# Queries and keys of a head group computed together by seven half products, with x parked in DRAM

## The reference

```python
cond = silu(c)
sh1, sc1, g1, sh2, sc2, g2 = split(cond @ w_ada + b_ada, 6)
h = rms_norm(x, norm_mix) * (1 + sc1) + sh1
y = dilated_mixture_attention(h, attn_w_in, attn_w_out)
x = x + g1 * y
h = rms_norm(x, norm_ffn) * (1 + sc2) + sh2
x = x + g2 * conv_ffn(h, ffn_w_up, ffn_conv_w, ffn_conv_b, ffn_w_down)
return rms_norm(x, norm_final)
```

## Time and profile before

| | |
|---|---|
| median of 3 runs | 942.18 us (941.74 to 942.84) |
| the profiled execution | 943.8 us, its span 942.0 us |
| TensorE (PE) busy | 922.9 us, 98%, 5828 matmuls |
| weight loads (PEld) | 797.4 us, 85% |
| VectorE (DVE) | 579.1 us, 61% |
| ScalarE (ACT) | 445.5 us, 47% |
| GpSimd (POOL) | 51.2 us, 5% |
| granted TensorE clock | 0.997 of full speed |
| DMA | 121.4 MB, 129 GB/s in the mean |

### The profile page before, as it was taken

The page is one execution under the profiler, slowest core; times in us unless marked ns, Lnnn a source line. Parts: engine busy times, 40 slices in busy tenths (PEclk is TensorE's granted clock), DMA queues, the critical chain, the costliest instruction groups (busy, mean ns, idle before and its releaser), DMA issues.

```text
span 942.0 us, 16200 instructions
## 1 busy us (share of the span) xinstructions
PE 922.9 (98%) x5828; PEld 797.4 (85%) x5828; DVE 579.1 (61%) x1261; ACT 445.5 (47%) x810; POOL 51.2 (5%) x75
## 2 busy tenths in 40 slices
PE   7999999999999999999999999999999999999995
PEld 6688888888888888888888888889999999888884
DVE  3444664745746557457565667888888888633325
ACT  7245435435344444453444555555666556432222
POOL 2000000000000000000000001411112111000000
PEclk9999999999999999999999999999999999999998
DMA  9865442343415332334242222367888876522302
GB/s 307 255 192 144 134 135 85 95 135 112 134 50 150 115 115 85 115 112 135 67 135 68 67 64 72 107 153 188 187 192 178 186 183 144 179 90 89 111 0 90
DMA packets 166528, 121.38 MB, mean 129 GB/s; under 512 B 4662, under 2 KB 149198, under 8 KB 166478
## 3 DMA queue, kind: packets, MB, share of 16 engines
q1 hardware_dynamic: 161088, 111.17, 39.1%
q0 software_dynamic: 5184, 9.44, 6.7%
q10 hardware_dynamic: 206, 0.08, 0.0%
HBM read 109.13 MB, written 2.10 MB: 118 GB/s over the span
## 4 chain that ended last, share of the span: by engine, by line
PE 90%; DVE 4%; DMA 2%; SPq 1%; ACT 1%; POOL 1%; issue 1%; DVEq 0%; POOLq 0%; ACTq 0%
PE bank L786 13%; PE bank L788 13%; PE bank L787 13%; PE bank L998 6%; PE bank L996 6%; PE bank L999 6%; PE bank L1045 4%; PE bank L1047 4%; PE bank L1046 4%; PE bank L870 3%; PE bank L846 3%; PE bank L813 2%; PE bank L879 2%; PE bank L806 1%; PE bank L881 1%; PE bank L880 1%
## 5 line engine op out<-in xcount | busy, mean ns | idle before, releaser
L1412 DVE TENSOR_TENSOR wl<-raw,wh 128x1024 fp32r<-128x1024 f32 (+1 forms) x127 | 150.5, 1185 | 176.9 <-ACT wh L1103 175.9
L786 PE MATMUL bank<-hh,wl 128*128 128x512 f32 x544 | 215.2, 396 | 0.0
L788 PE MATMUL bank<-hl,wh 128*128 128x512 f32 x544 | 212.0, 390 | 0.0
L787 PE MATMUL bank<-hh,wh 128*128 128x512 f32 x544 | 211.8, 389 | 0.0
L1103 ACT ACTIVATE wh<-raw 128x1024 fp32r<-128x1024 f32 (+1 forms) x127 | 130.4, 1027 | 60.3 <-PE bank L1047 50.9
L786 PEld LDWEIGHTS bank<-hh,wl 128*128 128x128 f32 x544 | 102.1, 188 | 23.9 <-issue 2.7
L788 PEld LDWEIGHTS bank<-hl,wh 128*128 128x128 f32 x544 | 102.1, 188 | 21.7
L787 PEld LDWEIGHTS bank<-hh,wh 128*128 128x128 f32 x544 | 102.2, 188 | 20.1
L996 PE MATMUL bank<-th,wl 128*128 128x256 f32 x304 | 84.8, 279 | 1.0 <-ACT p_copy L1280 0.9
L998 PE MATMUL bank<-th,wh 128*128 128x256 f32 x304 | 85.4, 281 | 0.0
L999 PE MATMUL bank<-tl,wh 128*128 128x256 f32 x304 | 85.1, 280 | 0.0
(11 more groups left out here) (221 smaller groups left out, 1600.2 us busy)
## 6 DMA issues: line engine op xcount, KB each, us to landing
raw<-in_attn_w_in SPq DMA_DIRECT2D x72, 512.0 KB, 3.8
ada_raw<-in_w_ada SPq DMA_DIRECT2D x16, 1024.0 KB, 5.4
raw<-in_ffn_w_up SPq DMA_DIRECT2D x25, 512.0 KB, 4.1
sums<-in_ffn_w_up SPq DMA_DIRECT2D x36, 256.0 KB, 3.3
raw<-in_ffn_w_down SPq DMA_DIRECT2D x17, 512.0 KB, 3.3
sums<-raw POOLq DMA_DIRECT2D x27, 256.0 KB, 4.9
ada<-in_w_ada SPq DMA_DIRECT2D x16, 256.0 KB, 6.8
raw<-in_attn_w_out SPq DMA_DIRECT2D x8, 512.0 KB, 3.6
```

The lines of the kernel that those rows point to most:

```text
L786: nc.tensor.matmul(bank[:], wl[:, slot, t], xh[:, t], start=(t == 0), stop=False)
L787: nc.tensor.matmul(bank[:], wh[:, slot, t], xh[:, t], start=False, stop=False)
L788: last = nc.tensor.matmul(bank[:], wh[:, slot, t], xl[:, t], start=False, stop=(t == KT - 1))
L1412: nc.vector.tensor_tensor(dst, src, high.bitcast(F32), ALU.subtract).then_inc(done, 1)
```

## The change

1. **Blocks instead of q and k strips.** In pairs 1 to 7 the six strips of q and k become three blocks, one per group, of seven products each (`block`, `block_product`). The three value strips stay, and come first. Pair 0 stays in strips.
2. **Weight sums.** For each block, `pair_sum` holds four half tiles: two are loaded from the keys' weights and added to by DMAs on GpSimd's queue, two are made by DVE (`sum_pair`). They are split into high and low part like the other weights (`split_block`: SUM0, DIRECT, SUM1 of 1024 elements and LAST of 512 per partition).
3. **Input forms.** `token_forms` makes four forms of h (1024 elements a partition each) in the first pair on DVE, and ACT and DVE split them into `mh` and `ml`.
4. **Space.** `mh` lies where `xT` lay. So `xT` is written to DRAM (`x_held`, 2 MB) behind the loads of the first pair, and read back in four DMAs after the last block; the attention's residual add waits for these (`x_back`). `q_t` and `k_t` have one buffer instead of two, the output's copy uses `p_t` instead of `o_a`, and there is a fourth raw tile, `raw_3`.
5. **Order.** All programs are written out for the seven pairs. The attention of the pair before is called from `visit` between products. Each product writes one of two halves of the two `proj` banks, and so waits for ACT's copies (`copy_block`, `take_block`) and DVE's additions (`add_block`).
6. **Prologue.** The first chunk's modulation is done between the transposes of x, ACT copies its rows before the first weight split, and the dummy transposes become 5 + 12, 10 and none, where there were 16, 16 and 10.

The core of the diff:

```diff
-QKV_STRIPS = PAIRS * STRIPS
+QKV_STRIPS = STRIPS + GROUPS * (PAIRS - 1)
+BLOCKS = GROUPS * (PAIRS - 1)
...
+        def block_banks(g):
+            bank, other_bank = unit_bank(GROUPS + g), unit_bank(GROUPS + g + 1)
+            return bank[:, 0:HALF], other_bank[:, HALF:T], other_bank[:, 0:HALF]
...
+            sp.wait_ge(start_taken, KT)
+            sp.dma_start(x_held, xT[:]).then_inc(x_saved, 16)
...
+            sp.wait_ge(block_prod, PRODUCTS * BLOCKS)
+            sp.wait_ge(x_saved, 16)
+            for i in range(KT // 2):
+                sp.dma_start(xT[:, 2 * i:2 * i + 2], x_held[:, 2 * i:2 * i + 2]).then_inc(x_back[i], 16)
...
+                    pool.wait_ge(pair_in[0], 16 * (i + 1))
+                    pool.wait_ge(raw_in[r_two], 16 * count_two)
+                    nc.gpsimd.dma_start(pair_sum[:, 0], raw_of(r_two)[:, HK:KT], accum_op=ALU.add).then_inc(pair_added[0], 16)
...
+            pe.wait_ge(start_taken, KT + 2)
+            hold(5)
             start_columns(0)
-            pe.wait_ge(start_taken, KT + 2)
-            hold(16)
-            start_highs((0, 1), range(RING))
+            hold(12)
+            for s in range(RING):
+                start_highs((0, 1), (s,))
             start_modulation(1)
             start_lows((0, 1), range(RING))
             start_columns(1)
-            hold(16)
+            hold(10)
...
             start_lows((2, 3), (2, 3))
-            hold(10)
...
+            def block(n, g, visit):
+                i = block_of(n, g)
+                r, q, z = block_banks(g)
+                early, late = slice(0, HALF), slice(HALF, T)
+                pe.wait_ge(block_l[DIRECT], i + 1)
+                if g == 0:
+                    pe.wait_ge(strip_taken, strips_before(n) + 2)
+                else:
+                    pe.wait_ge(block_added, 3 * i)
+                block_product(r, 0, 0, hh[:, 0:HK, early], hl[:, 0:HK, early], True, False)
+                visit(g, 1)
...
+                block_product(q, 1, 0, mh[:, 0], ml[:, 0], True, False)
+                pe.wait_ge(block_copied, 3 * i + 1)
+                block_product(r, 1, 1, mh[:, 1], ml[:, 1], False, False)
+                pe.wait_ge(block_copied, 3 * i + 2)
+                block_product(z, 0, 1, hh[:, HK:KT, early], hl[:, HK:KT, early], False, True)
+                visit(g, 4)
+                pe.wait_ge(block_l[SUM1], i + 1)
+                pe.wait_ge(block_copied, 3 * i + 3)
+                block_product(r, 2, 0, mh[:, 2], ml[:, 2], False, False)
+                visit(g, 5)
+                pe.wait_ge(block_added, 3 * i + 1)
+                block_product(q, 2, 1, hh[:, HK:KT, late], hl[:, HK:KT, late], False, True)
+                pe.wait_ge(block_l[LAST], i + 1)
+                pe.wait_ge(block_added, 3 * i + 2)
+                block_product(r, 3, 0, mh[:, 3], ml[:, 3], False, True)
...
+            def sum_pair(n, g):
+                nc.vector.tensor_tensor(pair_sum[:, 1], pair_sum[:, 0], one[:, 0:HK], ALU.add).then_inc(pair_sums, 1)
+                dve.wait_ge(pair_sums, 2 * i + 1)
+                nc.vector.tensor_tensor(pair_sum[:, 3], one[:, HK:KT], pair_sum[:, 1], ALU.add).then_inc(pair_sums, 1)
```

The order of DVE's program in a pair (`take_group` copies transposed values, `take_probs` probabilities, `weigh` scales them, `read_ada` does steps of the w_ada product):

```diff
+            def pair(n):
...
+                sum_pair(n, 0)
+                split_block(split_l, n, 0, SUM0, block_l, wl)
...
+                mask_scores(n, 2)
+                mask_scores(n, 3)
+                split_block(split_l, n, 0, DIRECT, block_l, wl)
+                read_ada(n, (4, 5))
+                split_block(split_l, n, 0, SUM1, block_l, wl)
+                take_group(n, 0)
+                if n > 1:
+                    low_output(n - 1)
+                read_ada(n, (6, 7))
+                split_block(split_l, n, 0, LAST, block_l, wl)
+
+                mix_first(n, 4)
+                add_block(n, 0, 1)
+                sum_pair(n, 1)
+                split_block(split_l, n, 1, SUM0, block_l, wl)
+                add_block(n, 0, 2)
+                split_block(split_l, n, 1, DIRECT, block_l, wl)
+                mix_second(n)
+                add_block(n, 0, 3)
+                split_block(split_l, n, 1, SUM1, block_l, wl)
+                weigh(range(4))
+
+                split_block(split_l, n, 1, LAST, block_l, wl)
+                add_block(n, 1, 1)
+                take_group(n, 2)
+                take_ada(n)
+                take_probs(n, 0, True)
+                take_probs(n, 1, True)
+                sum_pair(n, 2)
+                add_block(n, 1, 2)
+                split_block(split_l, n, 2, DIRECT, block_l, wl)
+                add_block(n, 1, 3)
...
```

ACT's program in the same stretch:

```diff
+                exponentials(n, 2)
+                take_strip(before + 1, "v", 1, unit_bank(1), v_t[:, (n + 1) % 2])
+                split_block(split_h, n, 0, DIRECT, block_h, wh)
+                exponentials(n, 3)
+                pair_low_ready(n, 0)
+                split_block(split_h, n, 0, SUM1, block_h, wh)
...
+                for k in (1, 2, 3):
+                    copy_block(n, 0, k)
+                exponent_of_mix(n)
+                split_block(split_h, n, 1, SUM0, block_h, wh)
+                split_block(split_h, n, 1, DIRECT, block_h, wh)
```

More of the change, by code:

```diff
@@ L288, in y_bank, with first_bank @@
             return banks[(3, 7, 0, 1, 2, 6, 5, 4)[o]]
[L290 to L301, removed]
+        SUM0, DIRECT, SUM1, LAST = range(4)
+        def first_bank(s):
+            return banks[s] if s in (2, 3) else proj[s % 2]
@@ new lines, in v_slot_free, with block_slot_free @@
+        def v_slot_free(n, g):
+            if n == 1:
+                return strip_done, (4, 7, STRIPS + 1)[g]
+            return block_prod, PRODUCTS * (block_of(n, 0) - 1) + (3, 4, 7)[g]
+        def block_slot_free(n, g, kind):
+            before = strips_before(n)
+            if g == 0 and kind != SUM1:
+                return strip_done, {SUM0: 8 if n == 1 else before + 1, DIRECT: before + 2, LAST: before + 3}[kind]
+            if g == 0 and n == 1:
+                return strip_done, STRIPS
+            return block_prod, PRODUCTS * (block_of(n, g) - 1) + {SUM0: 3, DIRECT: 4, SUM1: 6, LAST: 7}[kind]
@@ new lines, in wait_block_read, with load_out @@
+            def wait_block_read(n, g, part):
+                i = block_of(n, g)
+                sp.wait_ge(block_l[LAST if part else DIRECT], i + 1)
+                sp.wait_ge(pair_sums, 2 * (i + 1))
+                sp.wait_ge(pair_added[1 - part], 16 * (i + 1))
+            def load_out(o):
+                load_raw(out_raw(o), w_o[:, :, P * o:P * (o + 1)])
+            sp.wait_ge(start_taken, KT)
+            sp.dma_start(x_held, xT[:]).then_inc(x_saved, 16)
+            sp.wait_ge(hl_done, KT)
@@ new lines, in block_product @@
+            def block_product(out, slot, late, xh, xl, start, stop):
+                for t in range(HK):
+                    high, low = wh[:, slot, HK * late + t], wl[:, slot, HK * late + t]
+                    nc.tensor.matmul(out, low, xh[:, t], start=(start and t == 0), stop=False, skip_group_check=True)
+                    nc.tensor.matmul(out, high, xh[:, t], start=False, stop=False, skip_group_check=True)
+                    last = nc.tensor.matmul(out, high, xl[:, t], start=False, stop=(stop and t == HK - 1),
+                                            skip_group_check=True)
+                last.then_inc(block_prod, 1)
@@ L1214, in _ @@
+            first_pair()
+            for n in range(1, PAIRS):
+                pair(n)
+            last_pair()
             nc.scalar.activation(warm[:, 0:1], ones[:, 0:1], ACT.Sqrt)
```

878 lines of the change are left out of this document (601 added, 277 removed).

## The result

The kernel after takes 946.26 us (median of 7 runs, 945.77 to 948.67), the kernel before 942.84 us in the same series (7 runs, 941.74 to 944.49): a ratio of 1.0038, 95% interval 1.0028 to 1.0047. The change makes the kernel 0.4% slower. I had forecast 937.5 us, range 924 to 946.

The account below looks back on a forecast made before the run. PE's own work was taken to set the time. Pairs at -3.2 us and prologue at -1.5 us summed to -4.7, span 942.0 to 937.3, median 937.5 us; forecast's own range 932 to 940.3, eight in ten 924 to 946.

Parts of the forecast that it names:

- the two stalls of a pair: Block 0: PE waits 1.2 us on add 2 before P7, 1.0 us on add 3 before block 1's P1.
- the chain ahead of block 0: DVE must finish mix_first by P4's end, 25.2 us into the pair; forecast to end at 25.5, without slack.
- -0.45 us a pair, seven pairs -3.2 us: Pairs 1 to 7: PE work -2.85 us, stalls +2.2, restarts +0.2 a pair.
- the walk: Step-by-step timing of block 0 in DVE's queue order from P4's end, giving stalls of 1.2 and 1.0 us.
- rival 4: Next to nothing gained: stalls of 2.6 to 3.2 us a pair, 940.3 to 944.1 us; chance 0.12.
- PE's own work: Per pair, 252 matmuls of 256 columns replace 144 of 512; with one more break, 2.85 us less from 62.03.
- the mark of being wrong: A stated sign: the forecast is wrong if products lie more than 0.12 us apart; 0.118 was expected.
- rival 2: DVE falls behind, the chain before mix_first having no slack: 949 us by the bound; 0.19 together with the late-DMA rival.
- the prologue, -1.5 us: Before the first strips: fewer dummy transposes save 1.5 us, bounds -2.3 and 0; gains in front are given back.
- The slow bound of the walk: No DVE or ACT instruction starts before the one ahead ends: stalls 3.8 us, period 63.2 us, +8.3 us in all.
- my 0.69 on faster: Chance given to the whole kernel measuring faster; same had 0.12, slower 0.19.

Follow-up runs that it names:

- before_parked: Kernel before, with only the writing of x to DRAM and reading it back added: 943.2 us, ratio 1.0000 to the kernel before.
- reorder3: reorder2 with pair 1 as in reorder: 930.16 us, ratio 0.9864 to the kernel before.
- h_shift: Kernel after with hh and hl 64 bytes further in SBUF: 947.07 us, ratio 1.0038 to the kernel before.
- forms_shift: Kernel after with mh, ml, th, tl, fh, fl 32 bytes nearer the start of SBUF: 944.1 us, ratio 0.9996 to the kernel before.
- old_prologue: Kernel after with the prologue of the kernel before and its order of first splits: 946.45 us, ratio 1.0033 to the kernel before.
- mix_later: Kernel after with mix_second behind add 3 in DVE's queue in block 0: 940.08 us, ratio 0.9967 to the kernel before.
- reorder: Kernel after with block 0's adds on DVE ahead of what PE doesn't yet need, ACT's order changed too: 933.19 us, ratio 0.9887 to the kernel before.
- reorder2: reorder with second half sum and ACT's copy of product 1 moved earlier, and in pair 1 mix_first earlier, w_ada steps 4 to 7 later: 938.89 us, ratio 0.9958.
- best: reorder2 with SP's half-sum load ahead of its wait for the w_ada product in pair 1, and forms_shift's placement: 927.2 us, ratio 0.9821 to the kernel before.
- add2_first: Kernel after with add 2 ahead of the split of SUM0 on DVE in block 0: 948.86 us, ratio 1.0059 to the kernel before.
- final: reorder3 with the placement of forms_shift: 927.2 us, ratio 0.9814 to the kernel before.

## Why the prediction was wrong

**Right.** The count of matmuls; the two stalls of a pair, their place, their cause and that none hangs on a DMA (the Trainium skill's rule on the port shared by DVE and GpSimd, SBUF — State Buffer, SBUF: two separate sides, did not come to bear with DVE at 79%; no run here shows whether these DVE operations are of the kind it speaks of); DVE at 79% for a forecast 80%; add 1 at 0.32 us after P4 (239.65), so the chain ahead of block 0 was just in time as walked; x parked at no cost (before_parked, shown).

**Wrong: the term "-0.45 us a pair, seven pairs -3.2 us", by its size.** Pairs 2 to 7 cost +0.3 us each. Between the forecast and that lie 0.75 us, in two halves.
- The stalls. With reorder3's 59.50 us as the period of the same products without a wait, they cost 2.8 us; I had 2.4. I priced add 1 and add 3 at the 0.42 us of the up-projection's add. They write q in another token order and take 0.63 and 0.61, while add 2 takes 0.42 as its row says. The prediction drew just this line for ACT's copies, 0.38 plain and 1.12 in order, and not for DVE's adds. As everything stands in one queue, the 0.21 us of add 1 make add 2 late and lengthen the stall on it; the stall on add 3 is longer by add 3's own 0.19. PE also starts 0.14 us behind the end of an add (243.89 to 244.03), where the walk has 0.04. So the stalls are 1.52 and 1.15 us where the walk has 1.21 and 0.97. By themselves they belong to rival 4 (2.6 to 3.2 us a pair, 940.3 to 944.1 us), which was given 0.12; the terms below put the result above it.
- PE's own work. 59.50 us stand against the forecast's 62.03 - 2.85 = 59.18. The matmuls that read hh and hl lie 0.1195 us apart in the mean instead of 0.1178: 108 a pair, 0.2 us; the forms at 0.1183, 144 a pair, 0.07. The pitch of the earlier trace rows belonged to operands at other addresses, which h_shift and forms_shift show to matter. The prediction named 0.12 us as the mark of being wrong; the first product of a block lies on it.

**Wrong: pair 1 was counted as one of seven.** It took 64.1 us for 62.5, 2.0 us more than the forecast's 62.1. It has four w_ada steps ahead of the masks, where the others have one; the masks end 2.3 us later behind the scores than in pair 3, and mix_first ended at 115.5 us, too late for P6: three waits (0.67, 1.68 and 0.99 us) in the place of two, 1.0 us more. I had walked one pair, and had said myself that the chain there had no slack. This is the mechanism of rival 2, in one pair of seven. It accounts for 1.0 of the 2.0 us; 0.75 are those of any pair, and 0.25 stay open. That the four steps are the cause is read from the trace; no run moved them alone.

**Wrong: the prologue, -1.5 us.** It was -0.4 in the profile and nothing in old_prologue. I subtracted the dummy transposes, and had the new order in front down as a gain that is given back at the second modulation. But the interrupted transposes of x end 1.9 us later than in old_prologue (16.80 for 14.86); three of the four parts of the first modulation are done by then, and still the first matmul on hh comes 1.1 us later and that on tile 2 0.3 us later, where the forecast had it 0.3 us earlier.

**Not in the prediction:** 0.4 us in the last attention, 1.4 us that come back behind it (-1.1 in the output tiles, +0.75 in the up-projection, -1.1 in the down-projection).

In sum 6 x 0.75 + 2.0 + 1.1 + 0.4 - 1.4 = 6.6 us on the spans, which is the distance from -4.7 to +2.0. The forecast was a small difference of large terms, 20 us saved against 17 us of stalls. The two adds priced too low are 0.4 us a pair, 2.8 us: with them alone put right it would have been -1.9, so no one term turned its sign. The slow bound of the walk (63.2 us a pair) held it; my range, cut off 0.3 us below the result, and my 0.69 on faster did not.

**What decided it** is shown by mix_later and reorder: the load of the engines allows the gain. Against after, mix_later gets 7 us by moving six small operations, reorder 14 and reorder3 16. Against the kernel before, reorder3 is 13 us faster, of the 20 that the work alone promised.

## What to carry to other kernels

When an engine answers another one between its own long instructions, write the queue in the order in which the answers fall due, and put what nobody waits for behind them; a load share of 80% did not tell of it here. Look up the duration of each answer in the form that it has here, with its rearrangement; a fifth of a microsecond in such a chain is paid again in every period. Before moving work back in one queue, list who waits for its semaphore, the DMA queue too: in reorder2 that cost 7.8 us in one place.

## What the runs showed of the hardware

- **A wait can cost more than its length.** Waits of PE of 1.8 us (pair 1 of reorder), 2.0 (best) and 2.27 to 2.29 us (three in add2_first) were followed by 3.4 us in which the granted clock was at the 1.2 GHz level, about 1.5 us lost in the one reckoned out. In the wait of 7.8 us (reorder2) the clock fell at 133.6 us, before the wait was over, and stayed there until 143.9, 5.0 us behind its end. The 1.4 and 1.7 us of after were followed by no fall, and neither were four of the seven waits of add2_first (2.15 to 2.28 us). In the prologue of final the clock fell behind a wait of 1.35 us, and behind one of 1.33 us at the same place of after it did not. So the length of the wait alone does not tell them apart; what does was not tried.
- **The pitch of fp32r matmuls hangs on where the operands lie.** h_shift changes nothing else, and its product 1 went from 0.120 to 0.113 us a matmul. With 256 columns the pitch was 0.120 us, 0.118 or 0.113, nearly the same for one product of a block from pair to pair. The distances that follow are worked out from the order and sizes of the tensors in kernel.py, modulo 128 bytes. 0.113 to 0.1145 came with the moving operand 64 bytes from the weights (product 1 of h_shift, P2 and P3 of forms_shift, the output tiles of after), 0.120 with both at the same place (output tiles of before, product 1 of after), 0.118 with 32 bytes between. But P4 and P6 of h_shift stayed at 0.118, P4 of after lies at 0.1186, the long stream of the up-projection only went from 0.1183 to 0.1178 with forms_shift, and 512 columns became slower in h_shift where 256 became faster. So the distance is not the whole rule, which stays open. The Trainium skill (TensorE: Matmul & The Clock Gate, Wait — 56ns, not 53.3ns?) has 2.5 ns over N / 2.4 GHz for matmuls back to back, which makes an estimate of 109 ns for 256 columns; the best row here, 113 ns with a weight load for every matmul, is 4% above it.
